# Attention scores from 64-row matmuls of two heads, with q and k in whole tiles, and VectorE's side work placed after the next unit's maxima

## The reference

```python
c = jnp.cumsum(jax.nn.log_sigmoid(f_logit.astype(jnp.float32)), axis=1).transpose(0, 2, 1)
scale = dh ** -0.5
for i in range(S // Q_BLOCK):              # blocks of 128 queries
    q0, q1 = i * Q_BLOCK, (i + 1) * Q_BLOCK
    qb = q[:, :, q0:q1]
    kp, vp, cp = k[:, :, :q1], v[:, :, :q1], c[:, :, :q1]
    s = jnp.einsum('bhqd,bhkd->bhqk', qb, kp).astype(jnp.float32) * scale
    s = s + c[:, :, q0:q1, None] - cp[:, :, None, :]
    s = jnp.where(mask[None, None], s, -1e30)
    p = jax.nn.softmax(s, axis=-1).astype(v.dtype)
    outs.append(jnp.einsum('bhqk,bhkd->bhqd', p, vp))
```

## Time and profile before

| | |
|---|---|
| median of 3 runs | 1435.47 us (1435.26 to 1435.56) |
| the profiled execution, its own time | 1435.38 us |
| its span | 1433.4 us (about 2 us lie around it) |
| attention units | 336.7 to about 515 us of the span |
| matmul weight loads (PEld) | 1162.9 us busy |
| VectorE / ScalarE busy in 356 to 378 us | 18.63 / 18.33 of 22 us |
| granted TensorE clock | 0.999 of full over the span |

### The profile page before, as it was taken

The page is one execution under the profiler, slowest core; times in us unless marked ns, Lnnn a source line. Parts: engine busy times, 40 slices in busy tenths (PEclk is TensorE's granted clock), DMA queues, the critical chain, the costliest instruction groups (busy, mean ns, idle before and its releaser), DMA issues.

```text
span 1433.4 us, 19474 instructions
## 1 busy us (share of the span) xinstructions
PE 1410.4 (98%) x7026; PEld 1162.9 (81%) x7026; DVE 1007.4 (70%) x1460; ACT 644.3 (45%) x1216; POOL 558.4 (39%) x573
## 2 busy tenths in 40 slices
PE   8999999999899999999999999999999999999998
PEld 5878888887688888888888788888888888888886
DVE  7846495646877637877657887767777677795867
ACT  6545343535877653546443532233322322444445
POOL 5743243334545412013012654444444443354402
PEclk9999999999999999999999999999999999999999
DMA  8265264446332298314203113333322335883334
GB/s 212 54 128 119 53 137 99 74 85 210 111 118 90 75 283 193 112 57 127 63 6 136 60 61 105 110 111 110 110 100 93 109 111 198 305 283 99 91 103 147
DMA packets 108105, 173.71 MB, mean 121 GB/s; under 512 B 7485, under 2 KB 63313, under 8 KB 106474
## 3 DMA queue, kind: packets, MB, share of 16 engines
q1 hardware_dynamic: 98976, 148.17, 35.3%
q0 software_dynamic: 5408, 15.76, 4.3%
q10 hardware_dynamic: 3626, 8.54, 1.6%
HBM read 125.42 MB, written 42.30 MB: 117 GB/s over the span
## 4 chain that ended last, share of the span: by engine, by line
PE 87%; POOL 3%; DVE 3%; ACT 3%; DMA 2%; issue 1%; SPq 1%; DVEq 0%; ACTq 0%; POOLq 0%
PE ps L2354 27%; PE ps L2356 27%; PE ps L2355 27%; PE ps L2554 2%; PE ps L2563 1%; DMA w_raw<-in_w_xkv 1%; POOL w_lo L875 1%; PE ps L2592 1%; ACT prob L1340 1%; PE ps L2593 1%; DMA e_raw<-in_w_in 1%; SPq L667 1%; PE ps L2416 1%; DVE prob L1934 1%; PE ps L2729 0%
## 5 line engine op out<-in xcount | busy, mean ns | idle before, releaser
L2354 PE MATMUL ps<-t_lo,s_hi 128*128 128x512 f32 x308 | 119.9, 389 | 0.1
L2356 PE MATMUL ps<-t_hi,s_lo 128*128 128x512 f32 x308 | 119.8, 389 | 0.0
L2355 PE MATMUL ps<-t_hi,s_hi 128*128 128x512 f32 x308 | 119.8, 389 | 0.0
L2354 PE MATMUL ps<-h_lo_T,w_hi 128*128 128x512 f32 x256 | 100.5, 392 | 1.3 <-ACT u_t L1251 1.0
L1549 ACT ACTIVATE s_hi<-w_raw 128x512 fp32r<-128x512 f32 x77 | 48.7, 632 | 118.0 <-PE ps L2356 91.9
L1634 DVE TENSOR_TENSOR s_lo<-w_raw,s_hi 128x512 fp32r<-128x512 f32 x77 | 62.0, 805 | 56.3 <-ACT s_hi L1549 56.3
L2356 PE MATMUL ps<-h_hi_T,w_lo 128*128 128x512 f32 x256 | 99.7, 390 | 0.0
L2355 PE MATMUL ps<-h_hi_T,w_hi 128*128 128x512 f32 x256 | 99.6, 389 | 0.0
L1565 ACT ACTIVATE p_sb<-ps 128x512 f32<-128x512 f32 x22 | 13.0, 598 | 186.6 <-PE ps L2356 186.6
L2354 PE MATMUL ps<-hf_lo_T,w_hi 128*128 128x512 f32 x212 | 82.5, 389 | 0.0
L2355 PE MATMUL ps<-hf_hi_T,w_hi 128*128 128x512 f32 x212 | 82.5, 389 | 0.0
(11 more groups left out here) (403 smaller groups left out, 4373.9 us busy)
## 6 DMA issues: line engine op xcount, KB each, us to landing
w_raw<-hs_dram SPq DMA_DIRECT2D x77, 256.0 KB, 2.8
raw_p<-in_w_ffn_in SPq DMA_DIRECT2D x22, 512.0 KB, 4.6
w_raw<-in_w_ffn_in SPq DMA_DIRECT2D x22, 512.0 KB, 4.3
hs_dram<-h_sum SPq DMA_DIRECT2D x11, 1024.0 KB, 9.0
hs_dram<-hq SPq DMA_DIRECT2D x11, 768.0 KB, 7.1
wq_B<-in_w_ffn_out SPq DMA_DIRECT2D x8, 1024.0 KB, 7.6
raw_f<-in_w_in SPq DMA_DIRECT2D x14, 512.0 KB, 7.3
gate_dram<-c_st SPq DMA_DIRECT2D x28, 256.0 KB, 2.0
```

The costliest lines, as they stand in the source:

```text
L2354: nc.tensor.matmul(dst, w_h, x_l, start=start, stop=False, skip_group_check=onto)
L2355: nc.tensor.matmul(dst, w_h, x_h, start=False, stop=False, skip_group_check=onto)
L2356: return nc.tensor.matmul(dst, w_l, x_h, start=False, stop=stop, skip_group_check=onto)
```

## The change

It does two things. First, q and k lie in whole tiles of 128 rows (`q_hi`, `q_lo`, `k_hi`, `k_lo`), rows 0 to 63 being one head and 64 to 127 the other, and the scores are three matmuls of 64 rows for each head, written alternately for the two heads. The zeroed halves, the doubled `q1` with its DMAs, and half of the split instructions go: a quarter of q or k is one ScalarE and one VectorE instruction over 128 rows instead of two of 64 rows. TensorE waits for both heads' maxima of unit u-1 before the first score matmul of u, and both heads' `sc_done` are raised in the last two matmuls. Second, VectorE's side work of unit u moves behind the maxima of unit u+1 (before the reciprocals of u+1).

```diff
-SPLIT_HI = {1: (0, 0, 1), 2: (0, 1, 2), 3: (1, 0, 1), 4: (1, 1, 2), 5: (2, 0, 2), 6: (3, 0, 2)}
+SPLIT_HI = {1: 0, 3: 1, 5: 2, 6: 3}
...
-                if r >= 2:
-                    for a in range(2):
-                        own, other = slice(a * DH, (a + 1) * DH), slice((1 - a) * DH, (2 - a) * DH)
-                        sp.dma_start(q1[p % 2][a][other, half_of(i)].bitcast(FP32), q1[p % 2][a][own, half_of(i)].bitcast(FP32)).then_inc(q1_doubled, 16)
...
+            def side_work(u):
+
+                p, i = divmod(u, T)
+                if u in DEFER_DONE:
+                    last_pair(DEFER_DONE[u])
+                for m in MIXED_IN.get(u, ()):
...
+                if 2 * u in GATED_IN and 0 < i < 4:
+                    pool_gated(GATED_IN[2 * u])
+                if 2 * u + 1 in GATED_IN:
+                    pool_gated(GATED_IN[2 * u + 1])
+                if i < 4 and u < 3 * T and i - 1 in SPLIT_HI:
+                    e = SPLIT_HI[i - 1]
+                    qk_lo_of(p + 1, e, (qk_st if p else qk_first)[:, e % 2, :])
...
+                if u:
+                    side_work(u - 1)
...
-                    for a in range(2):
-                        if u == 12:
-                            pe.wait_ge(mix_lo, 6 + a)
-                        if u:
-                            pe.wait_ge(sc_biased, 2 * (u - 1) + a + 1)
-                        q1a, k1a, q2a = q1[p % 2][a], k1[p % 2][a], q2[p % 2][a]
-                        for c in range(0, i + 1, 4):
-                            n = min(4, i + 1 - c)
-                            keys = slice(c * P, (c + n) * P)
-                            dst = ps[:, 2 * a + c // 4, 0:n * P]
-
-                            nc.tensor.matmul(dst, q1a[:, tile_of(i)], k1a[:, keys], start=True, stop=False)
-                            last = nc.tensor.matmul(dst, q2a[:, tile_of(i)], k1a[:, keys], start=False, stop=True)
-                        last.then_inc(sc_done, 1)
+                    if u == 12:
+                        pe.wait_ge(mix_lo, 7)
+                    if u:
+                        pe.wait_ge(sc_biased, 2 * u)
+                    for c in range(0, i + 1, 4):
+                        n = min(4, i + 1 - c)
+                        keys = slice(c * P, (c + n) * P)
+                        for term, (q, k) in enumerate(((q_lo, k_hi), (q_hi, k_hi), (q_hi, k_lo))):
+                            for a in range(2):
+                                head = slice(a * DH, (a + 1) * DH)
+                                last = nc.tensor.matmul(ps[:, 2 * a + c // 4, 0:n * P], q[p % 2][head, tile_of(i)],
+                                                        k[p % 2][head, keys], start=term == 0, stop=term == 2)
+                                if term == 2 and c + n == i + 1:
+                                    last.then_inc(sc_done, 1)
```

More of the change, by code:

```diff
@@ L331, in build @@
         za = [place(f"za{m}", kb, [P, S]) for m, kb in enumerate((40, 44, 48, 52, 56, 60, 32, 180))]
-        q1 = [[place(f"q1_{i}{a}", (160, 88)[i] + 4 * a, [P, S], F32R) for a in range(2)] for i in range(2)]
-        q2 = [[place(f"q2_{i}{a}", ((168, 172), (96, 176))[i][a], [P, S], F32R) for a in range(2)] for i in range(2)]
-        k1 = [[place(f"k1_{i}{a}", (80, 100)[i] + 4 * a, [P, S], F32R) for a in range(2)] for i in range(2)]
+        q_hi = [place(f"q_hi{i}", kb, [P, S], F32R) for i, kb in enumerate((160, 88))]
+        q_lo = [place(f"q_lo{i}", kb, [P, S], F32R) for i, kb in enumerate((168, 96))]
+        k_hi = [place(f"k_hi{i}", kb, [P, S], F32R) for i, kb in enumerate((80, 100))]
+        k_lo = [place(f"k_lo{i}", kb, [P, S], F32R) for i, kb in enumerate((84, 104))]
         negc = [place(f"negc{i}", kb, [P, S]) for i, kb in enumerate((112, 116, 108))]
@@ L444, in build @@
         negc_masked, negc_plain = sem("negc_masked"), sem("negc_plain")
-        q1_doubled = sem("q1_doubled")
-        qk_hi, qk_lo, q2_zeroed, negc_loaded = sem("qk_hi"), sem("qk_lo"), sem("q2_zeroed"), [sem(f"negc_loaded{i}") for i in range(3)]
+        qk_hi, qk_lo, negc_loaded = sem("qk_hi"), sem("qk_lo"), [sem(f"negc_loaded{i}") for i in range(3)]
         sc_done, sc_biased, exp_ready, inv_ready, prob_ready = (
@@ L1195, in front_hi_of, with qk_hi_of @@
                 nc.scalar.activation(by_k(front_hi[n % RING1]), front_operand(g, q), ACT.Copy).then_inc(op_hi, 1)
-            def qk_hi_of(p, r, src, a0=0, a1=2):
+            def qk_hi_of(p, r, src):
                 which, h = divmod(r, 2)
[L1200 to L1206, removed]
+                nc.scalar.activation((k_hi if which else q_hi)[p % 2][:, half_of(h)], src, ACT.Copy,
+                                     scale=1.0 if which else DH ** -0.5).then_inc(qk_hi, 1)
             def quadrant_ready(g, q):
@@ L1797, in _, with qk_lo_of @@
             LESS_AT = {(7, P3): 0, (7, P7): 1, (8, P6): 2, (9, P2): 3}
-            def qk_lo_of(p, r, src, a0=0, a1=2):
+            def qk_lo_of(p, r, src):
                 which, h = divmod(r, 2)
-                if p:
-                    dve.wait_ge(qk_hi, 4 + 8 * p + (2, 4, 6, 8)[r] - (1 if a1 == 1 else 0))
-                else:
[L1805 to L1819, removed]
+                dve.wait_ge(qk_hi, 4 * p + r + 1)
+                if which:
+                    minus_hi(k_lo[p % 2][:, half_of(h)], src, k_hi[p % 2][:, half_of(h)], qk_lo)
+                else:
+                    nc.vector.scalar_tensor_tensor(out=q_lo[p % 2][:, half_of(h)], in0=src, scalar=DH ** -0.5,
+                                                   in1=q_hi[p % 2][:, half_of(h)].bitcast(FP32),
+                                                   op0=ALU.mult, op1=ALU.subtract).then_inc(qk_lo, 1)
             def spread_gain(h):
@@ L1921, in o_lo_of @@
                 minus_hi(o_lo[p][:], o_sb[:, p, :], o_hi[p][:], o_lo_ready)
+            def side_work(u):
[3 more added lines that the diff above has]
+                for m in MIXED_IN.get(u, ()):
+                    g, h = divmod(m, 2)
+                    dve.wait_ge(mix_hi, m + 1)
+                    nc.vector.scalar_tensor_tensor(out=d_lo[:, g, half_of(h)], in0=ps[:, MIX_BANK[m % 3], :],
+                                                   scalar=ps_scale[:, g:g + 1], in1=d_hi[:, g, half_of(h)].bitcast(FP32),
+                                                   op0=ALU.mult, op1=ALU.subtract).then_inc(mix_lo, 1)
+                if 2 * u in GATED_IN and 0 < i < 4:
[5 more added lines that the diff above has]
+                    qk_lo_of(p + 1, e, (qk_st if p else qk_first)[:, e % 2, :])
             for u in range(PAIRS * T + 1):
@@ L1947, in _ @@
                                             ALU.mult).then_inc(prob_ready, 1)
[L1948 to L1962, removed]
                 if u in (25, 26, 27):
@@ L2575, in _ @@
                 if u < PAIRS * T:
[L2576 to L2581, removed]
-                        if u == 12:
-                            pe.wait_ge(mix_lo, 6 + a)
-                        if u:
-                            pe.wait_ge(sc_biased, 2 * (u - 1) + a + 1)
-                        q1a, k1a, q2a = q1[p % 2][a], k1[p % 2][a], q2[p % 2][a]
-                        for c in range(0, i + 1, 4):
-                            n = min(4, i + 1 - c)
-                            keys = slice(c * P, (c + n) * P)
-                            dst = ps[:, 2 * a + c // 4, 0:n * P]
-                            nc.tensor.matmul(dst, q1a[:, tile_of(i)], k1a[:, keys], start=True, stop=False)
-                            last = nc.tensor.matmul(dst, q2a[:, tile_of(i)], k1a[:, keys], start=False, stop=True)
-                        last.then_inc(sc_done, 1)
+                    pe.wait_ge(qk_lo, 4 * p + 4)
+                    if u == 12:
[12 more added lines that the diff above has]
+                                    last.then_inc(sc_done, 1)
                 if u and i == 0 and u < PAIRS * T:
```

18 lines of the change are left out of this document (5 added, 13 removed).

## The result

The changed kernel takes 1460.82 us (1460.40 to 1461.47, 4 runs) beside 1435.51 us (1435.26 to 1436.71, 4 runs) of the kernel before on the same chip: 1.0174 times as long, interval 1.0162 to 1.0187. That is 25.3 us slower, where 15.7 were forecast; 1460.8 lies in the range 1438 to 1475. The profiled execution took 1461.11 us.

What follows compares the result with a forecast made beforehand. TensorE was taken as the bound: 1435.4 - 6.0 (scores) + 4.4 (mode changes) - 3.2 (fewer split instructions) + 20.5 (side work) = 1451.1 us, range 1438 to 1475.

Steps and rivals of the forecast that it cites:

- What bounds the kernel: Whole span: TensorE, busy 98%; only its own time or its waits count, and a new wait costs its whole length.
- Scores: Score matmuls: 64-row halves partly side by side, a gain of 6.0 us, between 2.2 and 8.4.
- halves and their loads side by side: Score matmuls: if both halves' matmuls and weight loads overlap, a piece takes three pitches, a gain of 8.4 us.
- halves by columns told of halves by rows: Values product: two heads in 64 columns each work at once, taken as evidence that score halves by rows would too.
- Mode changes: Ahead of 32 units' scores and behind about 12 without values: 44 changes at 0.1, a loss of 4.4 us.
- Fewer split instructions: Attention: 12 VectorE and 12 ScalarE instructions go, shortening TensorE's waits; a gain of 3.2 us, ends 0 and 5.8.
- Side work: Attention: later read-outs of bank 7, last pair and mixes make TensorE wait, a loss of 20.5 us, ends 14 and 22.
- the prediction's own last sign: Prediction is wrong if za releases TensorE for under 8 us in all, or TensorE waits somewhere not named.
- the formula 0.20 + 2M + 0.69 + 0.06: End of scores' pitch to product's fill: 0.20, two maxima of M each, 0.69 for the read-out, 0.06 for the semaphore.
- serial halves: Rival, score matmuls: 64-row matmuls run one after the other, a loss of 17.4 us, 1474.5 us; chance 0.13.
- the faster one: Rival, products' fills: waits for the read-outs hardly cost, under 8 us in all; 1429 us, chance 0.12.
- The dear mode changes: Rival, scores: 44 mode changes at 0.2 cost more than halves with loads one after the other give; 1459.3 us, chance 0.13.

Runs made afterwards that it cites:

- the experiment in one half: Kernel with 64-row scores and side work at its old place, but both heads' score matmuls reading rows 0 to 63: 1453.98 us, 1.0129.
- the kernel without the mode: Kernel with side work at its old place, each pair of 64-row score matmuls replaced by one matmul over all 128 rows: 1428.57 us, 0.9954.

## Why the prediction was right, and where it was off

- **What bounds the kernel:** right. TensorE's new waits cost at least their length, and nothing took them back after the attention.
- **Scores:** the bound "halves and their loads side by side", a gain of 8.4 us, is what the pitches show (0.23 and 0.11 a pair). I took 6.0, so the term is too small by 2.4. That halves by columns told of halves by rows is borne out, with the experiment in one half as its counter-check.
- **Mode changes:** 4.4 forecast. The trace shows 0.20 for an entry, 0.15 at the four units that begin with a 128-column pair, and 0.10 for an exit; the exits without values are 16, not 12: 28 x 0.20 + 4 x 0.15 + 16 x 0.10 = 7.8. The size was off because I took the entry's gap from the values, whose first matmul shows no long pitch. In time the kernel without the mode gains only 4.1 us, as other engines' lateness then holds TensorE up. By pitches, the scores' gain and the mode's loss leave 0.6.
- **Fewer split instructions:** 3.2 forecast. With the side work in place the kernel gains 2.8 in all, of which 0.6 is the scores', so about 2.2; worked out, not measured by itself.
- **Side work:** the mechanism is right, and so are eight of the nine places of a wait for `za`. The ninth, u = 14, was to have none, and the wait for the mixes at u = 11 (1.35 us) wasn't named: by the prediction's own last sign these places are wrong. The working let the maxima wait for the scores alone. At u = 14 the scores end at 407.46, but VectorE waited for GpSimd's `negc` and began its maxima at 408.38, some 0.7 us later than by the formula, and TensorE's wait is 0.70 us. No wait shows at u = 20 and 28, where 0.2 each were listed.
- **Side work, sizes:** the formula 0.20 + 2M + 0.69 + 0.06 gives 2.17 for 512 keys and 2.71 for 768; the trace has 2.26 (441.29 to 443.55) and 2.78 (454.20 to 456.98). Its 0.06 for the semaphore came from no row; from the end of the read-out (442.72 + 0.69) to the fill (443.55) the trace has 0.14. At 20.5 us the waits' total was nearly right: the move costs 28.1 us (1460.8 less 1432.7), and less the clock's part that is 22.5. Part of this is luck: the waits for the last pair and the mixes came to 7.6 us where 3.8 were listed, while the wait for maxima at u = 12 (2.04 us with the side work in place) went, which wasn't forecast.
- **The step that was mis-sized most:** the sum for the side work had no clock in it. Four stretches at half clock at 1.4 us are 5.6 us of the 28.1, and of the 9.6 between the forecast and the measured time. Among the rows I had only gaps of up to 1.4 us with the clock at 1.00, and I priced a gap of 2 us at its length.
- Together: 1435.5 - 8.4 + 7.8 - 2.2 + 22.5 + 5.6 = 1460.8. The sum closes by construction: the 2.2 and the 22.5 are remainders.
- **The rivals:** serial halves are excluded by the pitches and by the run in one half; the faster one by the nine waits for `za`. The dear mode changes were right in their part (7.8 of the 8.8 allowed), but not with loads one after the other.

## What to carry to other kernels

Before an instruction is moved behind another on its engine, look up who waits for its result, what that engine has to do until then, and what else the instruction ahead may wait for; idle time on the moved instruction's engine says nothing on it. A read-out that frees the only PSUM bank of the next product belongs ahead of work which can't start before the producer has gone on; what is wanted a unit later can go behind. And a wait of TensorE of about 2 us may cost 1.4 us more than its length, in one execution and not in the next.

## What the runs showed of the hardware

- Two 64-row fp32r matmuls in different halves of the array run side by side in full, loads included: 0.23 us a pair at 512 columns, 0.11 at 128. In one half two of them take twice that: 0.46 (406.48 to 406.94 in the run with both heads in one half) and 0.23.
- The halves don't need neighbours in the order: with head 1's first matmul three places behind head 0's first both start at 406.96; six places behind, it starts with head 0's third (409.62).
- An entry of the 64-row mode costs 0.20 us of pitch (a gap of 0.1 and a first pair of 0.34), an exit 0.10. They cost the same where only one half is at work at the start or the end (409.05 to 409.38, and 411.21).
- The granted clock fell to 1.2 GHz for some 3.4 us after four of seven waits of 1.8 to 2.3 us in the changed kernel, after 15 of 26 such waits in all traces, and after none of five that were filled with transposes. What decides between like waits stays open.
